# Attention scores of the 1,024-token request as three fp32r products instead of one fp32 product

## The reference, cut to what matters

```python
q = (_rmsnorm(cq, q_norm_w) @ w_uq).reshape(b, s, N_HEADS_ATTN, QK_NOPE_DIM + QK_ROPE_DIM)
q_rope = _rope(q_rope, cos[:, None, :], sin[:, None, :])
kv = (_rmsnorm(ckv, kv_norm_w) @ w_ukv).reshape(b, s, N_HEADS_ATTN, QK_NOPE_DIM + V_HEAD_DIM)
k_rope = _rope(kr, cos, sin)
sc = jnp.einsum('bqhd,bkhd->bhqk', qn, k_nope) + jnp.einsum('bqhr,bkr->bhqk', qr, k_rope)
p = jax.nn.softmax(sc.astype(jnp.float32) * scale, axis=-1).astype(v.dtype)
```

## Time and profile before

| | us |
|---|---|
| median of 3 runs | 2824.84 (2823.27 to 2828.7) |
| the profiled execution | 2824.95 |
| its span, first to last instruction | 2823.2 |
| short request's tiles and what is ahead of the long keys | to about 455 |
| long request's key stage | about 455 to 483 |
| long request's eight tiles | about 483 to 832 |
| output projection, router, experts | from about 837 |

### The profile page before, as it was taken

How to read it: one execution, slowest core, us unless ns; L and a number is a source line. 1 busy time by engine, 2 the same in 40 slices (tenths; PEclk the granted TensorE clock), 3 DMA queues, 4 the chain that set the end, 5 groups by cost and what they waited for, 6 DMA issues and landing times.

```text
span 2823.2 us, 51614 instructions
## 1 busy us (share of the span) xinstructions
PE 2720.0 (96%) x18382; PEld 2398.6 (85%) x18382; DVE 2138.8 (76%) x4073; ACT 1535.9 (54%) x2898; POOL 228.6 (8%) x222
## 2 busy tenths in 40 slices
PE   7999888999999969999999999999999999999997
PEld 6989655666677859999999999999999999999996
DVE  4565887767765687877877878878878788788787
ACT  4443546454453345555555565555556555555566
POOL 0000431212200000000000000000000000000000
PEclk9999999999999989999999999999999999999999
DMA  7211312122146447767767868778677777677685
GB/s 282 69 61 58 129 39 78 55 108 84 75 151 216 150 160 242 256 230 244 255 217 251 259 220 263 228 241 266 224 253 239 231 246 257 223 256 238 234 268 213
DMA packets 359946, 548.24 MB, mean 194 GB/s; under 512 B 14816, under 2 KB 287968, under 8 KB 359840
## 3 DMA queue, kind: packets, MB, share of 16 engines
q1 hardware_dynamic: 352448, 520.88, 53.6%
q0 software_dynamic: 7392, 25.96, 4.3%
HBM read 494.30 MB, written 52.49 MB: 194 GB/s over the span
## 4 chain that ended last, share of the span: by engine, by line
PE 59%; DVE 3%; ACT 1%; DMA 1%; issue 0%; ACTq 0%; POOLq 0%; SPq 0%; POOL 0%; DVEq 0%
PE banks L3368 26%; PE banks L3381 16%; PE banks L3369 12%; PE banks L3341 4%; DVE weights_low L3116 1%; PE banks L3324 1%; DMA slab_down<-w_down 0%; ACT weights_high L3000 0%; DVE h_or_keys_or_sums L3252 0%; DMA weighted<-residual 0%; DVE hidden_parts L3267 0%; ACT h_or_keys_or_sums L3053 0%; DVE hidden L3262 0%; DVE rows L3198 0%; DVE weighted L3198 0%
## 5 line engine op out<-in xcount | busy, mean ns | idle before, releaser
L3368 PE MATMUL banks<-rowsT_parts,weights_high 128*128 128x384 f32 x4096 | 1236.0, 356 | 3.1 <-DVE hidden_parts L3267 2.2
L3369 PE MATMUL banks<-rowsT_parts,weights_low 128*128 128x192 f32 x4096 | 1025.7, 250 | 0.0
L3369 PEld LDWEIGHTS banks<-rowsT_parts,weights_low 128*128 128x128 f32 x4096 | 781.1, 191 | 1.2
L3368 PEld LDWEIGHTS banks<-rowsT_parts,weights_high 128*128 128x128 f32 x4096 | 769.2, 188 | 7.5 <-issue 4.1
L3116 DVE TENSOR_TENSOR weights_low<-keys_or_w_out,weights_high 128x1024 fp32r<-128x1024 f32 x512 | 603.5, 1216 | 1.4 <-ACT weights_high L3000 1.4
L3000 ACT ACTIVATE weights_high<-keys_or_w_out 128x1024 fp32r<-128x1024 f32 x512 | 523.8, 1049 | 21.9 <-PEq L2371 21.9
L3026 ACT ACTIVATE h_or_keys_or_sums<-banks 128x192 f32<-128x192 f32 x512 | 165.7, 324 | 438.7 <-PE banks L3341 305.5
L3252 DVE TENSOR_TENSOR h_or_keys_or_sums<-banks,h_or_keys_or_sums 128x192 f32<-128x192 f32 x512 | 181.3, 354 | 288.8 <-ACT h_or_keys_or_sums L3026 287.2
L3381 PE MATMUL banks<-weights_high,hidden_parts 128*128 128x512 f32 x1512 | 397.5, 391 | 1.6 <-DVE hidden_parts L3267 1.6
L3381 PEld LDWEIGHTS banks<-weights_high,hidden_parts 128*128 128x128 f32 x1512 | 279.0, 188 | 57.2 <-issue 2.0
L3116 DVE TENSOR_TENSOR weights_low<-slab_down,weights_high 128x1024 fp32r<-128x1024 f32 x256 | 311.3, 1216 | 0.0
(11 more groups left out here) (407 smaller groups left out, 3754.9 us busy)
## 6 DMA issues: line engine op xcount, KB each, us to landing
keys_or_w_out<-w_gate SPq DMA_DIRECT2D x128, 1024.0 KB, 5.3
keys_or_w_out<-w_up SPq DMA_DIRECT2D x128, 1024.0 KB, 6.9
slab_down<-w_down SPq DMA_DIRECT2D x128, 1024.0 KB, 4.9
arena_attend<-w_ada SPq DMA_DIRECT2D x8, 2048.0 KB, 7.8
attention<-ssd_tiles SPq DMA_DIRECT2D x12, 992.0 KB, 8.3
ssd_tiles<-arena_inputs SPq DMA_DIRECT2D x24, 256.0 KB, 2.0
mixed<-attention SPq DMA_DIRECT2D x12, 512.0 KB, 2.8
residual<-arena_output SPq DMA_DIRECT2D x12, 512.0 KB, 2.6
```

What stands on the lines that cost most here:

```text
L3368: nc.tensor.matmul(out[:, 0:2 * CT], w_hi[:, u, block], x[:, k, :], start=k == 0, stop=False)
L3369: mm = nc.tensor.matmul(out[:, 0:CT], w_lo[:, u, block], x[:, k, 0:CT], start=False, stop=k == KD - 1)
```

## The change

The queries and keys of the long request are split into a high part (the value rounded to fp32r) and a low part (the rest). `k_parts` holds for each head 128 rows: the high part of the 64 plain key values in rows 0 to 63 and the low part in rows 64 to 127. The query's plain values are written twice, so that `q_high` and `q_low` have 128 rows as well. The rotary part has its own arrays of 96 rows, `k_rope` and `q_rope` (three copies of 32 rows, one of which is replaced by the low part on each side). A bank of scores is the sum of three fp32r products: `q_high` by `k_parts`, `q_low` by `k_parts`, and `q_rope` by `k_rope`. The short request keeps its fp32 products.

For this, ACT first copies a transposed piece from its PSUM bank to the high array, and then DVE subtracts that from the same bank and writes the low part; until both are done the bank isn't free. In the key stage ACT makes three such copies a tile and DVE three subtractions, the rotary key is transposed into bank 0, and `turn_c`, which writes that bank too, now waits for `kT_done`. In the tile loop the transposes of the next tile's query are four groups instead of two, in h = 4 to 7 (`turn_q` on PE, `take_high` on ACT, `take_low` on DVE, parts 0 to 3; parts 0 and 1 in `b_x`, parts 2 and 3 in `b_y`), each waiting for the `take_low` of the part ahead or for the bank, and `turn_y` waits for all four. The arrays of queries are single, where `qT` had two. The two query products are now of four heads each.

```diff
+    def rounded(self, name, start, *shape):
+
+        if name not in self.kept:
+            part = max(p for p in self.place if p <= start)
+            self.kept[name] = self.nc.alloc_sbuf_tensor_at(name, [P, *shape], F32R, offset=self.place[part] + 4 * (start - part))
+        return self.kept[name]
...
+def rope_thrice(eng, link, out1, out2, x1, x2, cos, sin, t):
+
+    eng.tensor_tensor(t[0], x1, cos, ALU.mult)
+    eng.tensor_tensor(t[1], x2, sin, ALU.mult)
+    eng.tensor_tensor(t[2], x2, cos, ALU.mult)
+    link(eng.tensor_tensor(t[3], x1, sin, ALU.mult))
+    a, b, c, d = (part.unsqueeze(2).broadcast_to([P, NH, 3, 16]) for part in t)
+    eng.tensor_tensor(out1, a, b, ALU.subtract)
+    return eng.tensor_tensor(out2, c, d, ALU.add)
...
+    k_parts, k_rope = core.rounded("k_parts", A_KT, NH, 1024), core.rounded("k_rope", A_KN, 1024)
     wuq, wukv = A.at(A_WUQ, 2, NH * DQK), core.early.at(E_WUKV, NH * (DN + DV))
-    kn = [A.at(A_KN + 768 * j, NH, DQK) for j in range(2)]
+    kn = [A.at(A_P + 1024 * j, NH, 2, DN) for j in range(2)]
+    kn_rope = [A.at(A_E + 1024 + 3 * DR * j, 3, DR) for j in range(2)]
...
-            nc.scalar.activation(kn[j][:, 0:4, 0:DN], kv[:, :, 0:DN], ACT.Copy)
+            nc.scalar.activation(kn[j][:, 0:4], kv[:, :, 0:DN].unsqueeze(2).broadcast_to([P, 4, 2, DN]), ACT.Copy)
...
-            nc.scalar.activation(kT[0:DQK, 0:4, bass.ds(i * P, P)],
-                                 core.ps[3][0:DQK, :].rearrange("p (h t) -> p h t", h=4), ACT.Copy).then_inc(kT_done, 1)
+            for half in range(2):
+                nc.scalar.activation(k_parts[:, 4 * half:4 * half + 4, bass.ds(i * P, P)], turned_nope(half), ACT.Copy
+                                     ).then_inc(kT_high, 1)
+            nc.scalar.activation(k_rope[0:3 * DR, bass.ds(i * P, P)], rope_bank, ACT.Copy).then_inc(kT_high, 1)
...
+            thrice = [t.unsqueeze(1).broadcast_to([P, 3, 16]) for t in rot]
+            nc.vector.tensor_tensor(kn_rope[j][:, :, 0:16], thrice[0], thrice[1], ALU.subtract)
+            nc.vector.tensor_tensor(kn_rope[j][:, :, 16:], thrice[2], thrice[3], ALU.add)
...
-            nc.vector.tensor_copy(kn[j][:, 4:8, 0:DN], kv[:, :, 0:DN])
+            nc.vector.tensor_copy(kn[j][:, 4:8], kv[:, :, 0:DN].unsqueeze(2).broadcast_to([P, 4, 2, DN]))
...
-            dve.wait_ge(k_turned, g + 1)
-            nc.vector.tensor_copy(kT[0:DQK, 4:8, bass.ds(i * P, P)],
-                                  core.ps[4][0:DQK, :].rearrange("p (h t) -> p h t", h=4)).then_inc(kT_done, 1)
+            for half in range(2):
+                dve.wait_ge(kT_high, i * 3 + (half + 1))
+                low = k_parts[64:128, 4 * half:4 * half + 4, bass.ds(i * P, P)]
+                ins = nc.vector.tensor_tensor(low, turned_nope(half)[64:128], low.bitcast(F32), ALU.subtract)
+            ins.then_inc(kT_done, 1)
+            dve.wait_ge(kT_high, i * 3 + 3)
+            low = k_rope[0:DR, bass.ds(i * P, P)]
+            nc.vector.tensor_tensor(low, rope_bank[0:DR], low.bitcast(F32), ALU.subtract).then_inc(kT_done, 1)
...
         def turn_c(g, i, j):
             pe.wait_ge(cn_done, g + 1)
             pe.wait_ge(cT_done, g)
+            if not isinstance(i, int) or i >= 3:
+                pe.wait_ge(kT_done, g * 2 - 4)
             nc.tensor.transpose(core.ps[0][:, 0:P], cn[j][:, QL:], core.ident).then_inc(turned, 1)
...
-                mm = nc.tensor.transpose(core.ps[3 + h // 4][0:DQK, h % 4 * P:(h % 4 + 1) * P], kn[j][:, h, :],
-                                         core.ident)
-            mm.then_inc(k_turned, 1)
+                nc.tensor.transpose(core.ps[3 + h // 4][:, h % 4 * P:(h % 4 + 1) * P], kn[j][:, h].rearrange("p a e -> p (a e)"), core.ident)
+            pe.wait_ge(cT_done, min(g + 3, NT) if isinstance(g, int) else g + 3)
+            nc.tensor.transpose(rope_bank, kn_rope[j].rearrange("p a e -> p (a e)"), core.ident).then_inc(k_turned, 1)
...
+    def query_heads(part, g):
+
+        return ((0, 4), (4, 8))[part] if of_long(g) else ((0, 5), (5, 8))[part]
+
+    def q_bank(part, ahead):
+
+        if ahead:
+            return (b_x, b_y, core.ps[2], core.ps[3])[part]
+        return (b_x, b_x, b_y, b_y)[part]
...
+                if of_long(g):
+                    made = b_x[:, 0:4 * DQK].rearrange("p (h e) -> p h e", h=4)
+                    nc.scalar.activation(q_twice[part], made[:, :, 0:DN].unsqueeze(2).broadcast_to([P, 4, 2, DN]), ACT.Copy)
+                    nc.scalar.activation(q_raw[:, h0:h1, :], made[:, :, DN:], ACT.Copy).then_inc(q_copied, 1)
+                    return
...
+        def take_high(part, g, ahead=False):
+
+            act.wait_ge(q_turned, g * 4 + (part - 7))
+            bank, half = by_head(q_bank(part, ahead)), part // 2
+            if part % 2 == 0:
+                nc.scalar.activation(q_high[:, 4 * half:4 * half + 4, :], bank, ACT.Copy).then_inc(qT_high, 1)
+            else:
+                nc.scalar.activation(q_rope[half][0:3 * DR], bank[0:3 * DR], ACT.Copy).then_inc(qT_high, 1)
...
+                    rope_thrice(nc.vector, order.link, q_thrice[:, :, :, 0:16], q_thrice[:, :, :, 16:], x1, x2, cos, sin, rot
+                                ).then_inc(q_roped, 1)
+                    return
...
+        def take_low(part, g, ahead=False):
+
+            dve.wait_ge(qT_high, g * 4 + (part - 15))
+            bank, half = by_head(q_bank(part, ahead)), part // 2
+            if part % 2 == 0:
+                hs = slice(4 * half, 4 * half + 4)
+                nc.vector.tensor_tensor(q_low[:, hs, :], bank, q_high[:, hs, :].bitcast(F32), ALU.subtract).then_inc(qT_done, 1)
+            else:
+                low = q_rope[half][DR:2 * DR]
+                nc.vector.tensor_tensor(low, bank[DR:2 * DR], low.bitcast(F32), ALU.subtract).then_inc(qT_done, 1)
...
+                if r and follows and h >= 4:
+                    take_high(h - 4, g + 1)
...
+                if r and follows and h >= 4:
+                    take_low(h - 4, g + 1)
...
+        def turn_q(part, g, ahead=False):
+
+            if part == 0:
+                pe.wait_ge(q_roped, g + 1)
+            elif part == 2 and not ahead:
+                pe.wait_ge(gated, g)
+            elif not ahead:
+                pe.wait_ge(qT_done, g * 4 + (part - 8))
+            bank = q_bank(part, ahead)
+            for n in range(4):
+                cols = slice(n * P, n * P + P)
+                if part % 2 == 0:
+                    mm = nc.tensor.transpose(bank[:, cols], q_twice[part // 2][:, n].rearrange("p a e -> p (a e)"), core.ident)
+                else:
+                    mm = nc.tensor.transpose(bank[0:3 * DR, cols], q_thrice[:, part // 2 * 4 + n].rearrange("p a e -> p (a e)"),
+                                             core.ident)
+            mm.then_inc(q_turned, 1)
...
+            if r and h == 0:
+                pe.wait_ge(qT_done, g * 4 - 6)
+            if r and (h == 4 or h == 1 and isinstance(g, int) and g == lo):
+                pe.wait_ge(qT_done, g * 4 - 4)
             for k0 in range(0, keys_n, 512):
                 if k0 and not (isinstance(g, int) and g == lo and h < 2):
                     pe.wait_ge(pT_dve, g * NH + (h - 1))
-                mm = nc.tensor.matmul(core.banks[:, h % 2 * 1024 + k0:h % 2 * 1024 + k0 + 512],
-                                      qT[j][0:DQK, h, :], kT[0:DQK, h, k0:k0 + 512], start=True, stop=True)
+                out, cols = core.banks[:, h % 2 * 1024 + k0:h % 2 * 1024 + k0 + 512], slice(k0, k0 + 512)
+                if not r:
+                    mm = nc.tensor.matmul(out, qT[j][0:DQK, h, :], kT[0:DQK, h, cols], start=True, stop=True)
+                else:
+                    nc.tensor.matmul(out, q_high[:, h, :], k_parts[:, h, cols], start=True, stop=False)
+                    nc.tensor.matmul(out, q_low[:, h, :], k_parts[:, h, cols], start=False, stop=False)
+                    mm = nc.tensor.matmul(out, q_rope[h // 4][0:3 * DR, h % 4, :], k_rope[0:3 * DR, cols], start=False, stop=True)
             mm.then_inc(scored, 1)
...
+            if more and r:
+                pe.wait_ge(qT_done, g * 4 + 2)
+            elif more:
...
+            if r and more:
+                pe.wait_ge(qT_done, g * 4)
...
+                for part in range(3):
+                    turn_q(part, lo, True)
                 pe.wait_ge(sem("kT_done"), 2 * NT)
+                turn_q(3, lo, True)
...
+                if r and more and h >= 4:
+                    turn_q(h - 4, g + 1)
```

60 lines of the change are left out of this document (41 added, 19 removed).

## The result

| | before | after |
|---|---|---|
| median, us | 2824.09 (2823.27 to 2828.7, 4 runs) | 2869.12 (2867.04 to 2871.45, 4 runs) |
| profiled execution, span | 2824.95, 2823.2 | 2869.96, 2868.2 |
| first `turn_k` of the long request | 463.03 | 466.46 |
| first score of the long request | 483.30 | 513.74 |
| from one `late_products` to the next | 42.83 | 45.28 |

The account below looks back on a forecast made before the run. PE looked like the bound by busy time, but the order of waits on ACT and DVE was taken to decide: 2824.95 + 18.0 (key ring) + 7.5 (clock) + 14.8 (tiles) = 2865 us, eight-in-ten range 2839 to 2888.

Parts of the forecast that it names:

- The ring in the keys: Key stage: `turn_c` waits for DVE's last subtraction, so a turn takes 5.40 us against 2.75; +18.0 us.
- The clock: Key stage: PE's clock low in two of five long turns and both short ones; +7.5 us, bounds 0 and +16.
- The first tile's queries: End of key stage: transposes lie under waits, and shorter scores give back 1.3 us of copies and subtractions; 0.
- The tile: Second half of a tile: DVE and ACT take turns and `turn_y` waits; 2.3 us longer a tile, tiles +14.8.
- The first and the last tile: Tile loop: seven tiles, the first included, lose +16.1 us together; the eighth prepares no query and gains about 1.3.
- The scores: Scores on PE: six fp32r products take 1.39 us; a free head saves 0.33, a held head's second bank 0.15.
- PE's bound holds: Rival, whole stage: waits hide, each tile saves 1.8 us, 14 in all, keys cost nothing; 2811 us, chance 0.06.
- Only the ring: Rival: only the key stage costs, 25.5 us, and the tile is as long as before; 2850 us, chance 0.16.
- the clock in both: Rival: the clock falls in the key stage and in the tiles' h = 7; 2884 us, chance 0.11.

Follow-up runs that it names:

- The bank of its own: Rotary key transposed into bank 5 instead of bank 0, ScalarE's last short-request output copy moved ahead of the keys, against the changed kernel: 2853.4 us, ratio 1.0091.
- the copies ahead of the exponentials: `take_high` put ahead of the next head's exponentials in iterations 4 to 7 of a long tile, against the changed kernel: 2846.5 us, ratio 1.0081.
- The run with filled waits: Ten unread identity products a key-stage turn into bank 5, ScalarE's last-output copy moved ahead of the keys, against the changed kernel: 2863.0 us, ratio 1.0131.
- one product less: Third (rotary) product of each bank of long-request scores left out, its preparation kept, against the changed kernel: 2860.2 us, ratio 1.0125.

## Why the prediction held, point by point

- **The place of the loss.** The sum was 18.0 + 7.5 for the key stage and 14.8 for the tiles; the trace has 27.0 and 15.2 + 0.4 - 1.4 = 14.2. The bank of its own took 14 us off, the copies ahead of the exponentials 20, each at the place named. That the sum of 2865 came within 4 us of 2869.1 has some luck in it, since it lacked the 3.4 us ahead of the stage, and errors in the tiles and in the clock's turns cancel.
- **The ring in the keys.** 5.40 us was 5.59. PE's part was as worked out (1.89 and 1.28), the part of copies and subtractions was mis-sized: from ScalarE's first copy to PE's next start 2.42 us instead of 2.17, since DVE starts 0.76 after the copy (not 0.6), and then takes 1.33 for the two and 0.33 for the third. Over five turns 1 us.
- **The clock.** 7.5 us was the right size and the wrong split (5.6 + 2.0 is 7.6). Four of the five long turns were low, not two, and one of the two short ones; but each long one mainly for its `expand`, since the clock came back with the transposes (1.00 from 474 on), so it cost 1.4 to 1.6 a turn, not 2.8. With about 1.5 in the last transposes that is about 7.5. The run with filled waits bears it out from the other side: 5.1 us less in the stage, though it adds its own products to the last two turns.
- **The first tile's queries.** They were put at 0. PE goes on behind the last key at 512.43, and the first score comes 1.31 later, where the sum had 0.25: about 1 us of the stage is theirs.
- **The tile.** 2.3 us more a tile was 2.45 (45.28 against 45.1 predicted), and PE idle ahead of `turn_y` by DVE's subtraction stood in all six. Of the handovers, DVE waits for ScalarE 0.83 us in h = 4, 1.12 in h = 5 and 6 and 0.63 in h = 7. What I hadn't listed is the growth of the second wait, that of the second bank for DVE's copy, from 0.6 to 1.5 us a tile: the prediction followed the chain of the maxima and so had its time without naming it on PE.
- **The first and the last tile.** The last was to gain 1.3 us for want of a query, and from `turn_y` of tile 10 it gains 1.31 (35.79 for 37.10). The six in between are 2.5 longer each, not 2.3. The first was to be 2.3 longer too and is 0.6 longer: before, the scores of its first two heads run at the half clock (6.89 us from 483.30 to 490.19, granted 0.50), and after the clock is back at 1.00 from 512 on, ahead of them. That would account for it, though no run isolates it. The prediction had named that half clock and not counted it in the tile. These errors of 1.7 and 1.1 us have opposite signs.
- **The scores.** Six products take 1.48 us in a free head, not 1.39: the first of a group has 0.31 to the next start and the others 0.23. The free head saves 0.24, not 0.33.
- **What the sum didn't have.** 3.4 us lie ahead of the first `turn_k`. The last `turn_y` of the short request is at 460.91 after and 456.27 before. In the other profiles, whose code is the same up to there, it stands between 455.6 and 460.5, with a granted clock of 0.93 to 0.96 from 334 to 455 where before has 0.97. So most of it looks like how the clock fell in that execution. Whether the changed kernel draws the lower clock there more often than the one before isn't settled, with one profile of each.
- **The rivals.** "PE's bound holds" falls by the run with one product less: 29 us of PE's work gone and 9 gained. "Only the ring" falls by the copies ahead of the exponentials, and "the clock in both" by the stretch at 1.00 in the tile loop. It wasn't far off: in the profiles with the bank of its own, with 10 small products and with one product less the clock did fall in the tile loop behind such a wait, once, once and four times, for 0.8 to 1.5 us each.

## What to carry to other kernels

Before giving an idle engine a step between two others, ask for whom it must be done and behind what it will stand in that engine's queue: here 0.6 us of copy cost 0.6 a tile in one iteration and 2.3 in three, and the order of two lines gave it back. A bank that two stages share ties them together; the wait that guards it costs what its longest user takes, in every turn. And work moved to GpSimd is paid by DVE where both read two operands out of SBUF, so look up in the trace what runs there at the time.

## What the runs showed that I had not expected

- After an idle time of PE of 2.3 to 2.8 us in the key stage the clock was at half for the next 3 us in four of five turns and full in the fifth (484.55), with the same idle time of 2.55. With 0.73 us of idle time a turn it never fell. In the profile of the kernel with the copies ahead the one full turn was the second (472.81). In the tile loop waits of 1.7 to 1.9 us were mostly followed by the full clock, and in three profiles now and then by the half. What decides isn't shown by any run.
- The clock came back while PE did nothing but transposes: from 507.94 to the first score it has no other work, and the granted clock is 0.50 from 508 to 511 and 1.00 from 511.5 to 512. What the prediction quotes from the Trainium skill ("TensorE: Matmul & The Clock Gate", Part 4: PE-mode transpose), that the full clock does not engage for transposes, isn't borne out here.
- The two additions beside GpSimd's products: 1.27 and 2.27 us for 0.69, and GpSimd's product 2.35 for 1.90.
- The rotary part on GpSimd takes 0.46 an operation of 128 columns and 1.00 for 384, against 0.28 and 0.56 on DVE.
